# Decay and rate products in pairs, half of the cumulated decays and the first exponentials moved forward

## The reference, cut to what matters

```python
r, k, v, xw, xa, xg = jnp.split(zs, ...)                 # 512, 512, 512, 64, 64, 128 columns
w = -jax.nn.softplus(-(p['w0'] + jnp.tanh(xw) @ p['w_up'])) - 0.5
decay = jnp.exp(-jnp.exp(w))                             # = exp(-exp(-0.5) * sigmoid(w0 + tanh(xw) @ w_up))
a = jax.nn.sigmoid(p['a0'] + xa @ p['a_up'])
g = jax.nn.sigmoid(xg) @ p['g_up']
kk = k * p['k_k']
kk = kk / jnp.maximum(norm of kk in each head, 1e-12)
k = k * (1.0 + (a - 1.0) * p['k_a'])
# scan over time, S is 64 x 64 in each of 8 heads:
sa = S @ (-kk)
S = S * decay + sa * (kk * a) + v * k
y = S @ r
...
bonus = sum(r * k * p['r_k']) * v                        # within a head
```

## Time and profile before

| | us |
|---|---|
| median of 3 runs | 1399.42 |
| lowest and highest | 1396.41, 1400.54 |
| profiled execution | 1398.44 |
| its span, first to last instruction | 1396.6 |
| TensorE busy in the span | 1146.1 (82%) |
| VectorE, ScalarE busy | 436.1, 238.7 |
| TensorE's mean granted clock | 0.926 of full |

### The profile page before, as it was taken

The page is one execution under the profiler, slowest core; times in us unless marked ns, Lnnn a source line. Parts: engine busy times, 40 slices in busy tenths (PEclk is TensorE's granted clock), DMA queues, the critical chain, the costliest instruction groups (busy, mean ns, idle before and its releaser), DMA issues.

```text
span 1396.6 us, 21853 instructions
## 1 busy us (share of the span) xinstructions
PE 1146.1 (82%) x9283; PEld 796.6 (57%) x9283; DVE 436.1 (31%) x797; ACT 238.7 (17%) x400; POOL 109.9 (8%) x97
## 2 busy tenths in 40 slices
PE   4999989998989999998999836878787887878740
PEld 2788876777568878866864333434344443444320
DVE  5000003675446667433323271111111111111137
ACT  3100011244311121021111101111111111111001
POOL 3000000000000000000001101111111111111103
PEclk9999999999799999999999957999999999999975
DMA  7342242222130112153554034999999999999951
GB/s 276 121 150 75 75 138 72 71 68 68 31 77 25 48 30 54 46 198 114 201 198 176 31 152 136 390 426 425 426 416 424 414 425 418 414 420 420 420 201 61
DMA packets 47164, 290.78 MB, mean 208 GB/s; under 512 B 9204, under 2 KB 11318, under 8 KB 34027
## 3 DMA queue, kind: packets, MB, share of 16 engines
q1 hardware_dynamic: 41922, 281.41, 51.9%
q0 software_dynamic: 5184, 8.54, 1.8%
HBM read 274.97 MB, written 24.23 MB: 214 GB/s over the span
## 4 chain that ended last, share of the span: by engine, by line
PE 62%; DMA 25%; DVE 5%; issue 2%; ACT 2%; DVEq 1%; SPq 1%; POOL 0%; POOLq 0%; ACTq 0%
PE psum L646 59%; DMA arena<-in_e_up 17%; DMA arena<-in_e_gate 5%; PE psum L651 3%; DVE arena L1423 3%; DVE arena L1426 2%; ACT arena L1182 1%; DMA arena<-in_w_mem_kv 1%; DMA arena<-scratch_x,arena 1%; DMA arena<-in_p_abm 0%; SPq L627 0%; DVEq L2021 0%; POOL arena L2034 0%; SPq L623 0%; DVE arena L1441 0%
## 5 line engine op out<-in xcount | busy, mean ns | idle before, releaser
L646 PE MATMUL psum<-arena 64*64 64x64 f32 (+8 forms) x8760 | 1077.3, 341 | 155.5 <-DMA arena<-in_e_gate 60.6
L646 PEld LDWEIGHTS psum<-arena 64*64 64x64 f32 (+4 forms) x8760 | 738.1, 153 | 471.8 <-issue 214.2
L1182 ACT ACTIVATE arena<-psum 128x512 f32<-128x512 f32 (+8 forms) x151 | 94.6, 648 | 684.4 <-PE psum L646 397.1
L1423 DVE TENSOR_TENSOR arena<-arena,psum 128x256 f32<-128x256 f32 (+3 forms) x136 | 74.5, 548 | 403.5 <-PE psum L646 210.1
L1423 DVE TENSOR_TENSOR arena<-arena 128x1024 f32<-128x1024 f32 (+17 forms) x168 | 125.7, 758 | 195.8 <-PE psum L646 164.1
L651 PE MATMUL psum<-arena 128*128 128x128 f32 (+4 forms) x523 | 79.3, 288 | 42.6 <-DMA arena<-in_mem_prompt 13.3
L651 PEld LDWEIGHTS psum<-arena 128*128 128x128 f32 (+4 forms) x523 | 59.0, 151 | 74.8 <-issue 49.0
L2034 POOL TENSOR_TENSOR arena<-arena 128x1024 f32<-128x1024 f32 (+1 forms) x15 | 37.1, 2474 | 517.0 <-DVE arena L1423 517.0
L1423 DVE TENSOR_TENSOR arena<-psum,arena 128x256 f32<-128x256 f32 (+4 forms) x85 | 47.0, 564 | 66.8 <-PE psum L646 66.4
L2077 POOL DMA_INDIRECT arena<-scratch_x,arena x32 | 32.7, 1023 | 300.9 <-DVE arena L1972 300.3
L1401 ACT ACTIVATE arena<-psum 128x256 f32<-128x256 f32 x32 | 12.3, 383 | 247.7 <-PE psum L646 247.7
(11 more groups left out here) (105 smaller groups left out, 155.7 us busy)
## 6 DMA issues: line engine op xcount, KB each, us to landing
arena<-in_e_gate SPq DMA_DIRECT2D x32, 2048.0 KB, 16.8
arena<-in_e_up SPq DMA_DIRECT2D x32, 2048.0 KB, 21.9
arena<-in_e_down SPq DMA_DIRECT2D x32, 2048.0 KB, 12.6
arena<-in_w_in SPq DMA_DIRECT2D x46, 512.0 KB, 4.0
scratch_gates<-arena SPq DMA_DIRECT2D x24, 260.0 KB, 4.1
arena<-scratch_gates SPq DMA_DIRECT2D x8, 780.0 KB, 4.9
arena<-in_p_abm SPq DMA_DIRECT2D x8, 640.0 KB, 5.9
scratch_x<-arena SPq DMA_DIRECT2D x8, 512.0 KB
```

The costliest lines, as they stand in the source:

```text
L646: return pe.matmul(out, a, b, start=start, stop=stop)
L1182: return act.activation(out, a, ACT.Copy)
L1423: return v.tensor_tensor(out, a, b, op)
```

## The change

The twelve groups become eight steps. A decay group and the rate group of the same `j` are issued together, alternating between the two row halves of the array, into four banks (0 to 3 or 4 to 7), with one semaphore for both. The four output-gate groups then alternate with the four key groups. Gate tile 11 moves ahead of the bonus products, into banks 6 and 7. The first two scans of VectorE stand ahead of the key products' results, the other two behind `bonus_in`. The three first exponentials stand behind the wide copy, ahead of the copy of gate tile 12, where they stood behind it.

```diff
 # TensorE
-            n = 0
-            for what in range(3):
-                for j in range(NJ):
-                    if n >= 2:
-                        pe.wait_ge(s["lora_sig"], n - 1)
...
+            for j in range(NJ):
+                if j == 1:
+                    pe.wait_ge(s["head_root"], 1)
+                if j >= 2:
+                    pe.wait_ge(s["lora_sig"], 2 * j - 2)
+                for h in range(2):
+                    cols = slice(h * NH, (h + 1) * NH)
+                    mm(bank(4 * (j % 2) + h, NH), wup[0:64, j * P:(j + 1) * P], th[0:64, cols])
+                    last = mm(bank(4 * (j % 2) + 2 + h, NH), wup[64:128, j * P:(j + 1) * P], xwa[64:128, cols])
+                last.then_inc(s["lora_mm"], 1)
+            for j in range(NJ):
+                pe.wait_ge(s["lora_sig"], 2 * j + 5 if j < 2 else j + 7)
+                for h in range(2):
+                    last = mm(bank(4 * (j % 2) + h, NH), gup[:, j * P:(j + 1) * P], xg_[:, h * NH:(h + 1) * NH])
+                last.then_inc(s["lora_mm"], 1)
+                if j == 0:
+                    pe.wait_ge(s["head_recip"], 1)
+                if j < 2:
+                    pe.wait_ge(s["lora_sig"], 2 * j + 6)
+                else:
+                    pe.wait_ge(s["prep_done"], j - 1)
+                for h in range(2):
+                    last = mm(bank(4 * (j % 2) + 2 + h, NH), const("sel8t", NJ, P)[0:HA, j, :], rnk[0:HA, h * NH:(h + 1) * NH])
+                last.then_inc(s["kk_bcast"], 1)
             pe.wait_ge(s["lora_sig"], 12)
             gate_tile(G_BONUS, G_BONUS % 2, G_BONUS // 2, 0)
+            pe.wait_ge(s["prep_done"], NJ)
+            gate_tile(G_SAMP, G_SAMP % 2, G_SAMP // 2, 6)
 
             pe.wait_ge(s["bonus_in"], 1)
             for j in range(NJ):
+                if j == 1:
+                    pe.wait_ge(s["gate_out"], G_SAMP + 1)
...
-            for k in range(G_SAMP, G_TILE):
...
+            k = G_SAMP + 1
+            gate_tile(k, k % 2, k // 2, 6)
+            pe.wait_ge(s["side_ready"], SIDE_SAMP)
 # ScalarE
+            for j in range(NJ):
+                act.wait_ge(s["lora_mm"], j + 1)
+                for what in range(2):
+                    b0 = 4 * (j % 2) + 2 * what
+                    r0 = (PR_W0, PR_A0)[what] + j
+                    act.activation(halves((sg, ah)[what][:, j, :]), psum[:, b0:b0 + 2, 0:NH], ACT.Sigmoid,
+                                   bias=prm[:, r0:r0 + 1]).then_inc(s["lora_sig"], 1)
...
             gate_take(G_BONUS, G_BONUS % 2, G_BONUS // 2, 0)
+            gate_take(G_SAMP, G_SAMP % 2, G_SAMP // 2, 6)
             act.wait_ge(s["side_turned"], SIDE_SAMP)
             copy(srow[0:B, :, :], bank(0, 6, C_A)[0:B, :, :]).then_inc(s["side_ready"], 1)
-            for k in range(G_SAMP, G_TILE):
-                gate_take(k, k % 2, k // 2, 6 * (k % 2))
-
+
+            act.wait_ge(s["decay_arg"], 1)
+            act.activation(Pinc, Lc[:, :, 0:P], ACT.Exp, scale=-DECAY)
...
+            k = G_SAMP + 1
+            gate_take(k, k % 2, k // 2, 6)
 
             act.wait_ge(s["prep_done"], 2 * NJ + 1)
             act.sem_inc(s["ry_ready"], 1)
 # VectorE
             v.reciprocal(rnk[0:HA, :], rnk[0:HA, :]).then_inc(s["head_recip"], 1)
+            for j in range(2):
+                v.wait_ge(s["lora_sig"], 2 * j + 1)
+                v.tensor_tensor_scan(Lc[:, j, :], const("reset"), sg[:, j, 0:T], 0.0, ALU.mult, ALU.add)
...
             last.then_inc(s["bonus_in"], 1)
+            for j in range(2, NJ):
+                v.tensor_tensor_scan(Lc[:, j, :], const("reset"), sg[:, j, 0:T], 0.0, ALU.mult, ALU.add)
```

More of the change, by code:

```diff
@@ L811, in _ @@
             pe.wait_ge(s["lora_act"], 1)
-            n = 0
-            for what in range(3):
-                for j in range(NJ):
-                    if n >= 2:
-                        pe.wait_ge(s["lora_sig"], n - 1)
-                    for h in range(2):
-                        cols = slice(h * NH, (h + 1) * NH)
-                        a, b_ = [(wup[0:64, j * P:(j + 1) * P], th[0:64, cols]),
-                                 (wup[64:128, j * P:(j + 1) * P], xwa[64:128, cols]),
-                                 (gup[:, j * P:(j + 1) * P], xg_[:, cols])][what]
-                        last = mm(bank(2 * (n % 2) + h, NH), a, b_)
-                    last.then_inc(s["lora_mm"], 1)
-                    n += 1
-                    if what == 1:
-                        if j == 0:
-                            pe.wait_ge(s["head_recip"], 1)
-                        else:
-                            pe.wait_ge(s["prep_done"], j)
-                        for h in range(2):
-                            last = mm(bank(4 + h, NH), const("sel8t", NJ, P)[0:HA, j, :], rnk[0:HA, h * NH:(h + 1) * NH])
-                        last.then_inc(s["kk_bcast"], 1)
+            for j in range(NJ):
[8 more added lines that the diff above has]
+                last.then_inc(s["lora_mm"], 1)
@@ L1295, in _, with halves @@
             block_exps(NT - 1, True)
+            def halves(ap):
+                return ap.rearrange("p (h n) -> p h n", h=2)
             act.wait_ge(s["head_sum"], 1)
             act.activation(rnk[0:HA, :].rearrange("p (h n) -> p h n", h=2), psum[0:HA, 6:8, 0:NH], ACT.Sqrt).then_inc(s["head_root"], 1)
-            n = 0
-            for what in range(3):
-                for j in range(NJ):
-                    act.wait_ge(s["lora_mm"], n + 1)
-                    src = psum[:, 2 * (n % 2):2 * (n % 2) + 2, 0:NH]
-                    dst = (sg, ah, gT)[what][:, j, :].rearrange("p (h n) -> p h n", h=2)
-                    if what < 2:
-                        r0 = (PR_W0, PR_A0)[what] + j
-                        last = act.activation(dst, src, ACT.Sigmoid, bias=prm[:, r0:r0 + 1])
-                    else:
-                        last = copy(dst, src)
-                    last.then_inc(s["lora_sig"], 1)
-                    n += 1
+            for j in range(NJ):
[5 more added lines that the diff above has]
+                                   bias=prm[:, r0:r0 + 1]).then_inc(s["lora_sig"], 1)
+            for j in range(NJ):
+                act.wait_ge(s["lora_mm"], NJ + j + 1)
+                b0 = 4 * (j % 2)
+                copy(halves(gT[:, j, :]), psum[:, b0:b0 + 2, 0:NH]).then_inc(s["lora_sig"], 1)
             act.drain()
@@ L1351, in tile_evictions @@
                 gate_take(i * 2 + (G_TILE + 1), (G_TILE + 1) % 2, i + (G_TILE + 1) // 2, 6)
-            act.wait_ge(s["decay_arg"], 1)
-            act.activation(Pinc, Lc[:, :, 0:P], ACT.Exp, scale=-DECAY)
-            act.activation(Pinv, Lc[:, :, 0:P], ACT.Exp, scale=DECAY)
-            act.activation(Pexc, Pexc, ACT.Exp, scale=-DECAY).then_inc(s["exps_made"], 1)
             with act.Fori(0, NT - 1) as i:
@@ L1595, in _ @@
             v.reciprocal(rnk[0:HA, :], rnk[0:HA, :]).then_inc(s["head_recip"], 1)
+            for j in range(2):
+                v.wait_ge(s["lora_sig"], 2 * j + 1)
+                v.tensor_tensor_scan(Lc[:, j, :], const("reset"), sg[:, j, 0:T], 0.0, ALU.mult, ALU.add)
             for j in range(NJ):
                 v.wait_ge(s["kk_bcast"], j + 1)
-                stt(halves(kk[:, j, :]), halves(kTr[:, j, :]), pcol(PR_KK, j), psum[:, 4:6, 0:NH], ALU.mult, ALU.mult).then_inc(s["prep_done"], 1)
+                b0 = 4 * (j % 2) + 2
+                stt(halves(kk[:, j, :]), halves(kTr[:, j, :]), pcol(PR_KK, j), psum[:, b0:b0 + 2, 0:NH], ALU.mult, ALU.mult).then_inc(s["prep_done"], 1)
             v.wait_ge(s["lora_sig"], 8)
@@ L1620, in _ @@
             v.tensor_copy(sstk[:, 5, :, :], rT[:, :, T:N]).then_inc(s["samp_stack"], 1)
-            for j in range(NJ):
-                v.tensor_tensor_scan(Lc[:, j, :], const("reset"), sg[:, j, 0:T], 0.0, ALU.mult, ALU.add)
             v.memset(SR[:, 0, :, :], 0.0)
```

8 lines of the change are left out of this document (2 added, 6 removed).

## The result

The changed kernel took 1376.12 us (median of 4 runs, 1375.78 to 1380.58) beside 1397.91 for the kernel before (4 runs, 1396.06 to 1400.54): a ratio of 0.985, with a 95% interval of 0.982 to 0.988. A second set of runs gave 1377.92 (5 runs, 1375.60 to 1380.75) beside 1394.01 (9 runs): 0.988, with 0.986 to 0.990. The profiled execution after took 1375.78, with a span of 1373.9.

The account below looks back on a forecast made before the run. TensorE was taken as the engine the others wait for from 354 to 416 us; 13.1 (first piece) + 4.7 (tile 10 to token tile) + 1.7 (clock) - .9 (load wait) = 18.6 gave 1380 us, range 1375 to 1388.

Parts of the forecast that it names:

- The first piece: Decay, rate, key and output-gate products on TensorE from 354.09: gate tile 10 starts at 368.2 instead of 381.34, 13.1 us gained.
- the third step: Third paired decay and rate step: TensorE waits 1.5 us for both sigmoids of the first step, ends at 358.4.
- the two bounds: Output-gate and key group at full clock: 1.01 us if all scales, 1.14 if the height change does not; 1.08 taken.
- I hold the height of the products for the cause, and pairs for the cure: Half-height products lower TensorE's clock from 358 for 20 us; pairing them on two row halves keeps it full.
- The 1390: Time if idle gaps lower the clock: pairing would not help, as the gap ahead of the third step grows to 1.5 us.
- The first rival: The clock falls all the same, at 358 or in the alternation with 8-row products: 10.3 us given back, 1390; chance .13.
- the full clock up to 370: Sign of being right in the changed kernel's profile: TensorE's clock at 1.00 from 354 to 370.
- By itself this move gives nothing: Moving gate tile 11 ahead of the bonus products only takes it from a place where two engines had to be waited for.
- The hole: TensorE's idle time ahead of the first token tile shrinks from 5.21 to .7 us, ended by ScalarE after tile 12's copy.
- The first token tile at full clock: With a .7 us hole ahead, the tile takes the second tile's 12.57 us instead of 14.26: 1.7 us gained.
- the wait for the load of gate tile 13: SyncE's load lands at 403.9, TensorE wants it at 403.05 in the first token tile: .9 us lost, 0 to 2.
- The sum: All terms together: 13.1 + 4.7 + 1.7 - .9 = 18.6 us, profiled execution 1379.8, median said as 1380.

Follow-up runs that it names:

- the rest alone: Changed kernel with the twelve groups of products in the old order; gate tile 11, scans and exponentials as changed: 1390.76 us, 0.996 of the kernel before.
- the keys on 128 rows: Changed kernel with the four key groups on all 128 rows of the array, the added weight rows being zero: 1377.58 us.
- all decays, then all rates: Changed kernel with all four decay groups first and then all four rate groups, the output gate and key alternation as changed: 1384.33 us.
- the load early: Changed kernel with the load of gate tile 13 and the store of tile 11 ahead of the samples' store on SyncE: 1377.49 us.
- the halves "apart": Changed kernel in whose four steps the rate products wait by a semaphore for the end of the decay products: 1381.67 us.
- the halves in blocks: Changed kernel with both decay products, then both rate products, within a step: 1378.66 us.

## Why the prediction was right, step by step

TensorE's pauses among the half-height products, in the kernel before, in the rest alone and in the changed kernel:

```profile
356.85 3.60 PE L646 MATMUL psum<-arena 64*128 64x260 f32 x11 [0.73 <-ACT arena L1307]
```

```profile
355.49 6.78 PE L646 MATMUL psum<-arena 64*128 64x260 f32 x17 [0.73 <-ACT arena L1310]
```

```profile
354.54 2.32 PE L646 MATMUL psum<-arena 64*128 64x260 f32 x16 [1.31 <-ACT arena L1310]
```

- **The first piece** (13.1 predicted, 27.25 - 14.20 = 13.05 measured) held in each term: pairs at the price of one pass, a wait of 1.3 ahead of the third step (1.5 predicted), 1.08 for a group of the alternation. With no change of height a group takes (368.14 - 361.02) / 8 = .89 us (361.02 is the start of the alternation in the run with the keys on 128 rows), so the change costs .18 at full clock, between the two bounds that the prediction had (.12 and .25).
- **"I hold the height of the products for the cause, and pairs for the cure"** is the step whose reason failed in part. The old order was profiled twice, in the kernel before and in the run of the rest alone, and the clock fell in both, 4.1 and 3.8 us in, with a pause of .73 us behind the first two decay groups. The changed kernel has a longer one, of 1.31 us, among its pairs, and full clock behind it. So a pause alone doesn't explain the fall, and half-height products without a pause (all decays, then all rates) did not bring it in 6.4 us. The 8-row groups brought the clock down in every run that left them in turn with the output gate, but not in the two in which they are 128 rows high. I read this as both counting: the clock fell where half-height products and a pause came together, or where the products were very low. No run varied the pause alone, so that is argued and not shown. Nor are pairs the whole cure: of the 11.3 us that the new order of the products adds to the rest, 5.6 came without them. The Trainium skill ("TensorE: Matmul & The Clock Gate", HAM oscillation) puts falls of the clock down to idle gaps between bursts of matmuls. That agrees with the holes of 2.51 and 5.24 us, behind which the clock was low, and not with the fall in the alternation, where TensorE had no gap. The 1390 that the prediction drew from it does not follow from that section, in whose example the gaps are waits for a DMA longer than the 2 us of work ahead of each; here the gap ahead of the third step came (1.31), and the clock stayed full behind it.
- **The first rival** (the clock falls in the alternation) came true in its last part. It fell at the alternation's end and cost 15.85 - 14.24 = 1.6 us in gate tile 10, of the 10.3 that the rival had. So the full clock up to 370 that the prediction named as a sign of being right did not hold.
- **"By itself this move gives nothing"**, of gate tile 11, was wrong. The prediction's own times had the wait in them, with VectorE's block ending at 378.2: without tile 11 TensorE would reach the bonus products at 375.3 and wait 2.9. Once the first piece is short, the tile in this place is worth 2.5 us up to the first token tile, 1.9 over the stretch.
- **The hole** was .34, not .7, and VectorE ended it, not ScalarE, which the prediction had named as a sign of being wrong: `ry_ready` is raised without a wait for the end of tile 12's copy (the copy ran from 396.28 to 396.88, TensorE started at 396.59). From the first exponential to the tile it was 396.59 - 391.89 = 4.7, as predicted, so this chain decides by a few tenths, and the scans are worth the 2 us that the prediction gave them. From tile 10 to the token tile 3.2 us were gained (34.37 to 31.20), 4.7 predicted; the low clock in tile 10 is the difference. In the run of the rest alone, where tile 10 is at full clock, the same way took 409.42 - 379.87 = 29.55, beside the 29.7 predicted.
- **The first token tile at full clock** gave 1.7 (46.68 before, 44.98 with the load early), and the wait for the load of gate tile 13 took .56 of it back (.9 predicted).
- **The sum** of the stretch is 17.3 where 18.6 was predicted. That the first median lies only 3.9 under the 1380 is partly luck: the profiled execution beside it was 22.7 shorter than the one before, 5.4 of that in places that the change does not touch. The repeated runs, 16.1 below their kernel before, lie on the other side of the 18.6.

## What to carry to other kernels

Two products of half height on the two row halves cost one here, in either order of the list, and TensorE's clock stayed up with them where the same products one by one, with a short wait between, went with a fall. Taking the waits and the low products out from between them was worth as much as pairing them. Products of a few rows between full ones cost a change of height each time (.18 us) and brought the clock down behind them; zero rows that fill them up were cheaper, 3.3 us in the stretch. When a stretch gets shorter, ask which engine's result was hidden behind it: here VectorE's bonus input, which independent work (a gate tile) has to cover in its place. A total that wanders by 4 us with the clock long before the change is better judged by the stretch than by the median.

## What was not expected of the hardware

- Products of the other row half start beside those of the first across four passes in the list, and across a wait in the list where the next products are of the other half (eight weight loads in .80 us at 358.08, with the halves "apart").
- The same code between 203 and 217 us ran at a mean clock of 0.52, 0.63 and 0.76 in three executions, and moved all behind it by 4.6 us (351.19 to 355.78). What decides it was not tried. It is not the chip alone: of two runs on the same one, the halves in blocks and the keys on 128 rows, the mean was 0.76 in the first and 0.54 in the second.
- What exactly of rows and pauses brings the clock down stays open; the runs show only that neither alone accounts for all the falls and all the stretches at full clock.
